# RWKV-7 chunk loop: full-array transposes become products on 64x64 pieces, and a weight feed moves behind a wait

## What is computed

```
def step(s, inp):
    r_t, w_t, k_t, v_t, a_t, b_t = inp
    sa = jnp.einsum('bhij,bhj->bhi', s, a_t)
    s = s * w_t[:, :, None, :] + sa[..., None] * b_t[:, :, None, :] + v_t[..., None] * k_t[:, :, None, :]
    return s, jnp.einsum('bhij,bhj->bhi', s, r_t)
s_fin, y = lax.scan(step, s0, xs)
```

## Time and profile before

| | us |
|---|---|
| runs: median (lowest to highest, 3 runs) | 2183.52 (2180.32 to 2188.89) |
| the profiled execution / its span | 2186.08 / 2184.3 |
| PE busy / PEld / DVE / ACT / POOL | 1641.3 / 1226.1 / 627.5 / 374.4 / 180.7 |
| chunk loop, first group of warming products to the last sum | 295.0 to 487.6 |
| first level 1 of chunk 0; of chunk 1; of chunk 7 | 315.25; 337.14; 456.93 |
| reload of rows and feed of weights, first issue; transposes of the rows begin | 562.1; 581.7 |
| output product begins (it uses the weights) | 703.0 |

### The profile page before, as it was taken

How to read it: one execution, slowest core, us unless ns; L and a number is a source line. 1 busy time by engine, 2 the same in 40 slices (tenths; PEclk the granted TensorE clock), 3 DMA queues, 4 the chain that set the end, 5 groups by cost and what they waited for, 6 DMA issues and landing times. The chain is left out here.

```text
span 2184.3 us, 46140 instructions
## 1 busy us (share of the span) xinstructions
PE 1641.3 (75%) x20476; PEld 1226.1 (56%) x20476; DVE 627.5 (29%) x1584; ACT 374.4 (17%) x885; POOL 180.7 (8%) x166
## 2 busy tenths in 40 slices
PE   2999859981238934999980898999999526999990
PEld 2788738860225722666650676888787323666650
DVE  3100264435452152111117002000661431111117
ACT  0300323321020030111112010001660200111112
POOL 1000023410000022000004000000000120000004
PEclk7999969995578976999995998999999758999995
DMA  6020051001401136999956214442202184999953
GB/s 197 20 77 20 0 235 39 4 4 51 157 25 37 60 123 247 388 386 387 374 184 252 36 39 127 116 120 67 99 2 78 58 295 151 385 383 386 373 203 141
DMA packets 218733, 345.34 MB, mean 158 GB/s; under 512 B 69673, under 2 KB 116433, under 8 KB 218282
## 3 DMA queue, kind: packets, MB, share of 16 engines
q1 hardware_dynamic: 191354, 289.07, 37.5%
q0 software_dynamic: 9856, 33.81, 5.0%
q10 hardware_dynamic: 17328, 19.51, 2.7%
HBM read 295.56 MB, written 46.78 MB: 157 GB/s over the span
## 5 line engine op out<-in xcount | busy, mean ns | idle before, releaser
L1729 PE MATMUL bank<-ring_extra,xT 128*32 128x256 f32 x3456 | 194.4, 379 | 9.0 <-issue 9.0
L2123 PE MATMUL bank<-x,ring 128*128 128x256 f32 (+1 forms) x768 | 174.0, 387 | 3.4 <-issue 2.7
L426 PE MATMUL bank<-mix,ring 128*128 128x260 f32 x768 | 172.8, 386 | 4.3 <-issue 3.1
L1729 PEld LDWEIGHTS bank<-ring_extra,xT 128*32 128x32 f32 x3456 | 133.6, 110 | 65.6 <-issue 17.2
L426 PEld LDWEIGHTS bank<-mix,ring 128*128 128x128 f32 x768 | 146.1, 192 | 31.0 <-issue 8.8
L2123 PEld LDWEIGHTS bank<-x,ring 128*128 128x128 f32 x768 | 146.1, 192 | 28.1 <-issue 5.4
L1729 PE MATMUL bank<-ring,xT 128*32 128x256 f32 x2688 | 155.5, 385 | 7.5 <-issue 6.2
L1521 DVE TENSOR_TENSOR sg<-sg,bank 128x128 f32<-128x128 f32 x96 | 27.3, 285 | 377.7 <-ACT sg L1618 377.7
L1729 PEld LDWEIGHTS bank<-ring,xT 128*32 128x32 f32 x2688 | 101.7, 112 | 56.7 <-issue 15.2
L1818 PE MATMUL bank<-ring,x 128*128 128x256 f32 (+1 forms) x480 | 108.0, 386 | 2.5 <-PEq L2308 1.3
L1818 PEld LDWEIGHTS bank<-ring,x 128*128 128x128 f32 (+1 forms) x480 | 82.3, 173 | 28.3 <-issue 7.4
(11 more groups left out here) (364 smaller groups left out, 2177.8 us busy)
## 6 DMA issues: line engine op xcount, KB each, us to landing
ring_extra<-in_moe_w_gate SPq DMA_DIRECT2D x72, 512.0 KB, 9.5
ring_extra<-in_moe_w_up SPq DMA_DIRECT2D x72, 512.0 KB, 12.9
ring_extra<-in_moe_w_down SPq DMA_DIRECT2D x36, 1024.0 KB, 15.1
ring<-in_moe_w_gate SPq DMA_DIRECT2D x56, 512.0 KB, 9.2
ring<-in_moe_w_up SPq DMA_DIRECT2D x56, 512.0 KB, 12.6
ring<-in_moe_w_down SPq DMA_DIRECT2D x28, 1024.0 KB, 14.5
ring<-in_a_w_rkv SPq DMA_DIRECT2D x12, 1024.0 KB, 5.0
xe<-expert_in POOLq DMA_DIRECT2D x32, 384.0 KB, 8.0
```

What stands on the lines that cost most here:

```text
L426: ins = pe.matmul(ps[2 * (job % 4) + h][:, 0:HALF], w[:, kt, q * 128:(q + 1) * 128], m[:, kt, h * HALF:(h + 1) * HALF], start=kt == 0, sto ...
L1729: ins = pe.matmul(ps[i % 2][32 * q:32 * q + 32, 0:256], xT[:, kt, 32 * u:32 * u + 32], gate_up(w[kt // 2], kt % 2, q), start=kt == 0, stop ...
L2123: ins = pe.matmul(ps[2 * (job % 3) + h][:, 0:n], w[:, kt_, rr, :], z[:, kt_, lo:lo + n], start=kt_ == 0, stop=kt_ == 7)
```

## The change

In the chunk loop every turn becomes 16 products of 64x64 pieces with the identity. The turn of Tt is merged with the X group (`solve_x_and_turn_t`): X and turn alternate, in two halves that signal apart, so that masks and copies may start on half of the result. At level 1 the turned T has 64 columns, later 32. The turned halves go to banks 2 and 7, W and U go through the banks of the outputs (`wy`), so U now waits for `y_first`. V is turned from its source and the copies VS are dropped; Kt gets tiles of its own; Bt three buffers. ACT copies each turned tensor in two halves. `state_m` runs pair by pair. The preparation groups stand one level earlier, so does DVE's keeping of the scores. Two blocks of three warming products are added ahead of the loop, and one warming product in each level of chunk 0. In `reload_rows` the wait for the rows stands ahead of the weight feed.

The core of the diff:

```diff
-                def turn_t(k, l):
...
-                    for q in range(QUADS):
-                        ins = pe.transpose(ps[2][:, 128 * q:128 * q + 128], Tt[k % 2][:, q], ident)
-                    ins.then_inc(t_turned, 1)
+                def solve_x_and_turn_t(k, l):
...
+                    w = 64 if l == 1 else 32
+                    for x2 in range(2):
+                        t2 = 1 - x2
+                        right = eye[t2] if l == 1 else blocks(eye[t2], l, 0)
+                        for q in range(QUADS):
+                            for hp in range(2):
+                                x = pe.matmul(ps[x2][rows[hp], 32 * q:32 * q + 32], N[k % 2][rows[x2], hp, q], blocks(Tt[k % 2][rows[x2], q, hp], l, 1),
+                                              start=True, stop=True)
+                                t = pe.matmul(ps[t_bank[t2]][rows[1 - hp], w * q:w * q + w], Tt[k % 2][rows[t2], q, 1 - hp], right, start=True, stop=True)
+                        x.then_inc(x_ready[x2], 1)
+                        t.then_inc(t_turned[t2], 1)
...
                 def turn_v_b(c):
                     pe.wait_ge(ks_copied, 2 * c + 2)
-                    for q in range(QUADS):
-                        ins = pe.transpose(ps[3][:, 128 * q:128 * q + 128], VS[c % 2][:, 2 * q:2 * q + 2], ident)
-                    ins.then_inc(v_ready, 1)
...
+                    for src, lo in ((f["v"][:, :, at(c)], 0), (B[c % 2], 256)):
+                        for q, p2, hp in quads:
+                            ins = pe.matmul(ps[3 + hp][rows[p2], lo + 64 * q:lo + 64 * q + 64], src[rows[hp], 2 * q + p2], eye[hp], start=True, stop=True)
+                    ins.then_inc(vb_ready, 1)
...
                 def state_m(c):
...
-                    for q, p2, hp in quads:
-                        p = 2 * q + p2
-                        ins = pe.matmul(wy[p2][rows[hp], :, q], M[rows[hp], p], AR[c % 4][rows[hp], p], start=False, stop=q == QUADS - 1)
+                    for p in range(PAIRS):
+                        for hp in range(2):
+                            ins = pe.matmul(wy[p % 2][rows[hp], :, p // 2], M[rows[hp], p], AR[c % 4][rows[hp], p], start=False, stop=p // 2 == QUADS - 1)
                     ins.then_inc(wt_ready, 1)
...
                 def state_u(c):
-                    pe.wait_ge(w_copied, c + 1)
+                    pe.wait_ge(w_copied, 2 * c + 2)
+                    pe.wait_ge(y_first, 2 * c + 2)
...
                 scores_k(0)
+                warm(3)
                 turn_v_b(0)
+                warm(3)
+                turn_k(0)
...
                         if chain:
-                            turn_t(k, l)
-                            solve_x(k, l)
-                        if chain and l == 1:
-                            turn_k(k)
+                            solve_x_and_turn_t(k, l)
+                        if not state:
+                            warm(1)
+                        if prep and l == 1:
+                            scores_n(k + 1)
...
                 def mask(k, l):
-                    dve.wait_ge(x_ready, 5 * k + l)
                     for p2 in range(2):
+                        dve.wait_ge(x_ready[p2], 5 * k + l)
...
             sp.dma_start(rows[0:REQ, 4, :], io["x_sample"].rearrange("b s d -> (b s) d")).then_inc(got, 16)
+            sp.wait_ge(got, 80)
             feed.upto(sp, 0, TIME_OUT_END)
-            sp.wait_ge(got, 80)
```

More of the change, by code:

```diff
@@ L534, in time_mix_chunks @@
         B, K = [[by_pair(part(2, 2 * n + i, 512)) for i in range(2)] for n in range(2)]
-        Bt, Kt = [[by_quad(part(3, 2 * n + i, 512)) for i in range(2)] for n in range(2)]
+        Bt = [by_quad(part(3, i, 512)) for i in range(3)]
         BS = [by_head(part(4, i, 1024)) for i in range(2)] + [by_head(core.sb(own, "BS", [128, 1024])[:, :])]
@@ L657, in turn_v_b @@
                     pe.wait_ge(ks_copied, 2 * c + 2)
-                    for q in range(QUADS):
-                        ins = pe.transpose(ps[3][:, 128 * q:128 * q + 128], VS[c % 2][:, 2 * q:2 * q + 2], ident)
-                    ins.then_inc(v_ready, 1)
-                    for q in range(QUADS):
-                        ins = pe.transpose(ps[4][:, 128 * q:128 * q + 128], B[c % 2][:, 2 * q:2 * q + 2], ident)
-                    ins.then_inc(bt_ready, 1)
+                    for src, lo in ((f["v"][:, :, at(c)], 0), (B[c % 2], 256)):
+                        for q, p2, hp in quads:
+                            ins = pe.matmul(ps[3 + hp][rows[p2], lo + 64 * q:lo + 64 * q + 64], src[rows[hp], 2 * q + p2], eye[hp], start=True, stop=True)
+                    ins.then_inc(vb_ready, 1)
                 def turn_k(c):
-                    pe.wait_ge(v_copied, c + 1)
-                    for q in range(QUADS):
-                        ins = pe.transpose(ps[3][:, 128 * q:128 * q + 128], K[c % 2][:, 2 * q:2 * q + 2], ident)
+                    pe.wait_ge(bt_copied, 2 * c + 2)
+                    for q, p2, hp in quads:
+                        ins = pe.matmul(ps[3 + hp][rows[p2], 64 * q:64 * q + 64], K[c % 2][rows[hp], 2 * q + p2], eye[hp], start=True, stop=True)
                     ins.then_inc(kt_ready, 1)
@@ L690, in turn_w @@
                     pe.wait_ge(wt_copied, 2 * c + 2)
-                    if c:
-                        pe.wait_ge(u_copied, c)
-                    for q in range(QUADS):
-                        ins = pe.transpose(ps[7][:, 128 * q:128 * q + 128], WT[:, 2 * q:2 * q + 2], ident)
+                    for q, p2, hp in quads:
+                        ins = pe.matmul(wy[hp][rows[p2], 0, q], WT[rows[hp], 2 * q + p2], eye[hp], start=True, stop=True)
                     ins.then_inc(w_ready, 1)
                 def state_u(c):
-                    pe.wait_ge(w_copied, c + 1)
+                    pe.wait_ge(w_copied, 2 * c + 2)
+                    pe.wait_ge(y_first, 2 * c + 2)
                     pe.wait_ge(tt_new, 10 * c + 10)
@@ L821, in _ @@
                             keep_k(k + 1, 0)
+                        if chain:
+                            mask(k, l)
+                        if prep and l == 3:
+                            keep_b(k + 1, 1)
+                        if prep and l == 4:
+                            keep_k(k + 1, 1)
+                        if chain:
+                            add(k, l)
                         if state and l == 4:
@@ L872, in copy_w @@
                     act.wait_ge(w_ready, c + 1)
-                    act.activation(W, by_quad(ps[7][:, :]), ACT.Copy).then_inc(w_copied, 1)
+                    for hp in range(2):
+                        act.activation(W[:, :, hp], wy[hp][:, 0], ACT.Copy).then_inc(w_copied, 1)
                 def copy_u(c):
                     act.wait_ge(u_ready, c + 1)
-                    act.activation(U, by_head(ps[7][:, :]), ACT.Copy).then_inc(u_copied, 1)
+                    for hp in range(2):
+                        act.activation(U[:, hp], wy[hp][:, 0], ACT.Copy).then_inc(u_copied, 1)
                 exps(0)
@@ L884, in _ @@
                 copy_v(0)
+                copy_bt(0)
+                copy_kt(0)
                 for k in range(CHUNKS + 1):
```

109 lines of the change are left out of this document (45 added, 64 removed).

## The result

The changed kernel takes 2250.70 us (median of 4 runs, 2245.45 to 2253.77) against 2182.83 us before (4 runs): ratio 1.0304, 95% interval 1.0275 to 1.0333. It is 3% slower; forecast were 2174.3 and at most 2186. The profiled execution took 2253.77 us, 2252.0 of it span. (One of the four runs of experiment 4 fell in a slower state of the chip, 2614.88 us, and its figures are those of the other three.)

What follows compares the result with a forecast made beforehand. The prediction took the chunk loop to be bound by each level's dependency chain and PE's issue. Terms -11.7 - 1.7 + 0.8 + 4.8 - 3.4 + 2.0 = -9.2 us gave 2174.3 against 2183.52 us, range 2164 to 2186.

Steps and rivals of the forecast that it cites:

- What a group costs: TensorE groups of 16 products: 32 records at 14.4 ns, 0.46 us; a turn as products costs 0.26 us less.
- steady chunk: Chunks 1 to 6: levels sum to 17.34 us, with holes 18.02; -11.7 us over six chunks.
- the holes: PE idle with nothing to wait for, in the chunk loop: grow with instruction count from 0.49 to 0.68 us a chunk.
- rival B: Chunk loop: instruction supply limits, holes of 0.88 us per 256 instructions, total 2215 us; 8%, another 8% for half of it.
- The merged group: X group and turn of Tt together, each level: issues in 0.92 us, masks start on the first half.
- Rival A: M group: both row halves writing one bank serialise, 1.72 us becomes 3.4; +13.7 us, total 2188; 6%.
- Start, +4.8: Before the loop: two added warming blocks make scores to first X group 8.12 us, was 3.34; nothing hides it.
- Chunk 0, -3.4: First chunk: warming products keep the clock up, 18.5 us instead of 21.89; a loss of 1 to 3 otherwise.
- rival C: Clock falls in chunk 0 all the same, or D waits longer for a copy: 2178 to 2180 us; 20%.
- Tail, +0.8: Chunk 8, states only: U waits for both copies, +0.65 us, and +0.06 each for two halved copies.
- Reload, +2.0: Row reload: weights leave only after rows land, so their transfer and the stores end 2.0 us later, between 0 and 3.

Runs made afterwards that it cites:

- experiment 4: Changed kernel with the turn of Tt alone as four whole-array transposes again, ahead of the X group: 2213.53 us (median of three), ratio 1.0132 to the kernel before.
- experiment 2: Kernel before with unused products on idle TensorE: twelve long ones, then eight times 8 groups of 64 columns plus one long product: 2223.20 us, one run.
- experiment 6: Changed kernel with the M group alone in its old order of pieces: 2258.62 us, one run.
- experiment 7: Changed kernel without the two added blocks of warming products and the one in each level of chunk 0: 2250.72 us, ratio 1.0263 to the kernel before.
- experiment 8: Kernel before with one warming product added in each level of chunk 0: 2188.9 against 2191.13 us, ratio 1.0001.
- experiment 3: Kernel before with only the reload's wait for the rows moved ahead of the weight feed: 2191.94 against 2191.62 us, ratio 1.0014.

## Why the prediction was wrong

**The step that failed** is "What a group costs", as the steady chunk is built on it, together with the holes, which I took "to go with the number of instructions" and put at 0.68 us a chunk. I took 14.4 ns a record, read in one stretch of 0.46 us, as a price that adds up over a chunk. It is the pace of a burst. Over 256 instructions it is nearly twice that (3.46 us for 128 records, 27 ns, experiment 2). The holes were 44.8/6 = 7.5 us a chunk, not 0.68. The price of a hole in rival B, 0.88 us for each block, was too small as well, where 42 blocks came with 35 holes of 1.28 on average; B's mechanism was right, its 2215 was 36 us short, and I gave it 16% where the profile bore more.

**What I could have read.** PE busy for 115.03 of 119.79 us looked like an engine with its own work. Dividing the chunk by its instructions gives 3.97 us per 256, and the queue of instructions moved 31 packets in 119.79 us: with 1792 instructions the same pace gives 7 x 3.9 = 27 us. That the chunk of 19.48 us "ran as dense as the others with hardly any" was my argument against B; it only says that 5.03 blocks of such groups take as long as they take to arrive. The Trainium skill, Runtime: NRT & Kernel Launch, Instruction fetch mechanics, says that TensorE's memory holds 2048 instructions, is refilled in blocks of 256 by a queue of the sequencer's own, and that crossing a block is mostly hidden. The unit of 256 agrees with the trace; that it is mostly hidden does not: the 42 blocks that arrived in the six chunks came with 35 holes of 0.3 us or more.

**Steady chunk:** 17.34 us of chain and issue. Less the holes the chunk was 27.11 - 7.5 = 19.6, so this was 2.3 us low too, beside the holes. Level 2 of chunk 1, nearly free of them, lasts 3.40 us (354.89 to 358.29, 0.22 of it a hole) where I had 2.89, and its D starts 1.75 behind the merged group, not 1.56. A part of the 2.3 is the clock, 0.91 in these chunks, which I had not coupled to the holes. Another part is the merged group itself, below. I did not split the rest.

**The merged group** took longer to issue than the 0.92 us that I gave it: where no hole fell into it and the clock was full, the next group started 1.00 to 1.16 us behind its start in chunks 1 to 6 (0.93 once). Over five levels this is 0.4 to 1.2 us. Its masks start on each half, as predicted: 369.98 and 370.48 in one level. Rival A had nothing to it (experiment 6).

**Start, +4.8:** 8.13 us from the scores on, against 8.12. The terms are right. "Nothing hides it" is not: without the two blocks and with all else as changed it is 5.46 us (experiment 7), so they cost 2.7 of the 5.5 us that they last. No run shows that they and the products in chunk 0 buy anything in this kernel.

**Chunk 0, -3.4:** wrong in sign. It took 23.29 us from level 1 to level 1 where it was 21.89, and 3.2 us more with the beginning of chunk 1. Part of rival C came true: the clock was 0.50 from 330 to 332, after PE had been busy for 1.00 and 1.14 us of the two stretches of 2 us ahead, with a hole of 1.4 us in them. In the kernel before the clock was full throughout with the same product (experiment 8); what it is worth can't be told from the scatter of this chunk.

**Tail, +0.8:** 4.2. The wait for both copies is there: PE idles 1.49 us ahead of the U group instead of 0.92. Most of the rest is the clock at its lower level: the M group alone costs 1.6 more, and from 542 to 548 the clock is 0.50 again.

**Reload, +2.0:** 1.8, and 2.4 by itself (experiment 3). Right in mechanism and size: the weights leave when the rows have landed, and DMA moves 45 GB/s from 630 to 632.

## What to carry to other kernels

Count instructions, not only engine time: an fp32 product on a piece is four, a transpose two, and the four products that took the place of one transpose here are sixteen; 256 of them took 3.8 to 4.0 us to arrive in every loop here that had 1288 or more a chunk. Before making products smaller or more numerous, divide the stage's time by its instructions and look at the packets of the instruction queue; if the quotient is near that pace, the busy share of PE says nothing about room. Where the quotient is above it, as at 4.19, the chain and the engine's own work set the time, and fewer instructions give less. Holes of "issue" in the middle of a group, a fixed number of records apart, are the mark of it.

## What the runs showed of the hardware

- TensorE ran 128 fp32 records (256 instructions) in 1.95 us and then stood for 1.5 us, again and again, 3.46 to 4.0 us a block, while nothing but the instruction queue moved (8 GB/s). With others at 350 to 390 GB/s a pause grew to 5 us once.
- With the holes the granted clock was 0.91 in the six chunks and 0.50 (its level of 1.2 GHz) in most of the tail, where the kernel before had 1.00 in both. So missing instructions can cost more than the holes themselves; by how much, no run separates.
- Two row halves into one bank, one after the other: 269 ns a matmul and 1.59 us to issue the 32 weight loads of a group, as in the mixed order.
- What sets the 3.5 to 4.0 us stays open: the latency of one packet, the number that are under way, or the queue's place among the others. No run here tells these apart.
